# One core, two encoder layers: the order of a layer's steps written out anew, with weight steps of two units instead of four

## The chip, the cores and the metric

One core of a Trainium2 chip runs the whole program. The metric is the device time of one execution in microseconds (us), lower is better. The time before is 1046.75 us, the median of three runs (1046.62, 1046.75 and 1047.17).

The engines are named as in the profile: PE (TensorE, matrix products, with PEld for its weight loads), DVE (VectorE), ACT (ScalarE), POOL (GpSimd) and SP (SyncE, which here issues the DMAs of the weights). Each engine works through its own list of instructions in order. They meet at semaphores.

## The reference

The input x is 256 tokens by 1024 channels, float32. Two layers run one after the other, each of them:

```python
for l in range(DEPTH):                      # DEPTH = 2
    h = _rms(x, norm_g[l])
    p = einsum('bsd,de->bse', h, w_in[l])   # 1024 -> 11808 columns
    (a_qkv, a_a, a_b, a_z, b_qkv, b_z, c_q, c_k, c_v, c_z,
     d_q, d_k, d_v, d_i, d_f, d_o, d_z, gate_logits) = _split(p, PROJ_SIZES)
    y_a = gated DeltaNet, both directions, after a convolution over 5 tokens and SiLU
    y_b = attention in a neighbourhood of 16 columns, 8 heads of 64
    y_c = grouped-query attention with axial rotary, 4 heads of 128
    y_d = mLSTM, both directions
    proj = einsum('bsnw,nwd->bsnd', ys, w_branch[l])     # 4 branches, 512 -> 1024
    merged = sum over branches of sigmoid(gate_logits) * proj
    x = x + einsum('bsd,de->bse', merged, w_out[l])
```

Each mixer's output is multiplied by a SiLU gate of its own (za, zb, zc, zd). DeltaNet and mLSTM work in four chunks of 64 tokens. In DeltaNet every chunk needs the inverse of a 64x64 lower triangular matrix for each head.

## The kernel before

**Weights in units.** All weights of a layer, 232 blocks of 256 KB, are cut into "units" (`weight_plan`, line 213). SP loads a unit into one of six places of `ring` (line 1084). Since the products are made at a higher precision than one pass gives, every unit is split in two: ACT rounds it (`w_high`, line 1149) and DVE takes what is left (`w_low`, line 1475). PE then makes three products for each unit and each of two token tiles: lines 654, 655 and 656, six matmuls of 128x512 for most units. PARTS = 6 pairs of `w_high`/`w_low` exist, and LEAD = 4: a step that multiplies units k to k+n-1 on PE has ACT and DVE split units k+4 to k+n+3. Unit u can be split once unit u-6 has been used.

**Steps.** `order()` (line 127) makes one list of steps, and every engine goes through that same list (`run`, line 608), taking from each step its own part. A step ("proj", kind, arg, u, n) multiplies n units from unit u of a block on. Everything else is a small step. In the kernel before a block of eight units is made in two steps of four (SIZES = (4, 4), line 56), a branch block of four in one, and small steps lie between. The list depends on the position in `streamed`, on the integers in `add(...)` (so many weight steps here) and on `weave`, which mixes lists by fractions of a stretch. Because the list is common, the place of a small step in it sets where it stands on PE, ACT, DVE and POOL at once, and an engine that waits in one step holds up all of its later ones.

**At the end of a block** ACT and DVE have more to do (line 1212 and line 1701). After all but two of its splits ACT waits until the product of the first token tile is complete, takes it from PSUM, makes a split, waits for the second tile's product, takes it, and makes the last split. So the last split of a block's last step comes after PE has ended the whole block, and a small step that follows stands behind it on ACT and DVE. In the middle of a block nothing of this kind waits.

**The units in their order**: conv 0 to 3 are units 0 to 15, za 16 to 19 and 28 to 31, conv 4 and 5 units 20 to 27, c 32 to 47, zc 48 to 55, b 56 to 79, zb 80 to 87, d 88 to 103, o 104 to 111, zd 112 to 119, then for branches 0, 2, 1 and 3 and for two halves of the columns each a gate block of eight and a branch block of four (120 to 215), and out 216 to 231.

**Small steps that are spoken of below.**
- `conv.i`, `silu.i`: the convolution (DVE lines 1548 to 1552, ACT line 1271 and POOL lines 1951 to 1954 halve the work) and its SiLU (ACT 1277, DVE 1562). `a_turn.i` transposes the result on PE (line 648) and ACT takes it (1154).
- `gatecols`, `gatecols_turn`, `cols`: the gate columns of DeltaNet and mLSTM. gatecols_turn is a dialogue of DVE (1520 to 1540) and ACT (1253 to 1259, with a load of the table for Ln). cols: POOL makes eight copies into `sel` (line 1962), PE sums them (lines 780 to 783) once `selected` is 8, ACT takes exp, DVE makes terms (1567).
- `rope`: POOL only. Four copies (line 2043) and four products (2047) that make the rotary tables. The user is c_rotate.
- `a_norm`, `a_scale`, `a_qkt`, `a_kkqk`, `rows.s`: DeltaNet's norms and its decay matrices. rows.s is a chain PE (793), DVE (1593, 1595), ACT, POOL (1991), DVE (1597, 1599), and for s = 0 and 1 the first inverse (1612 to 1618).
- `solve0.s`, `t1.s.n`, `update.s.n`: the solve by levels n = 1 to 5, for chunks 0 and 1 together, then 2 and 3. POOL masks (2003), PE (831), ACT takes (1154), PE (842, 847), DVE subtracts (1630, at the last level 1633).
- `uw.s`, `qd.s`, `scan_v.s`, `scan_o.s`: the scan over chunks. scan_o ends with two products for the state (912) which wait until ACT has emptied the bank of the output (1154).
- `c_prep` to `c_out`: grouped attention; `c_rotate.t` is DVE work (1754 to 1767). `b_square`, `b_prep`, `b_turn_in`, `b_score`, `b_turn`, `b_mix`, `b_sum`, `b_out`: neighbourhood attention.
- `d_rows`, `d_prep`, `d_m`, `d_step.s`, `d_turn.s`, `d_scan.s`, `d_den`, `d_sum`, `d_gate`, `d_out`: mLSTM. d_step.s is DVE (1867), ACT (1415), DVE (1870). d_turn.s transposes what it makes.
- `x_out.t` puts the finished branch of x = a, b, c, d on PE for transposing; `y_parts.n` splits it as a weight is split; `merge_turn`, `merged` prepare the last product.

## Time and profile before

| | |
|---|---|
| median of three runs | 1046.75 us |
| the profiled execution, its own time | 1044.77 us |
| its span, first to last instruction | 1042.9 us |
| PE busy | 916.5 us, 88% of the span |
| DVE busy | 676.0 us, 65% |
| ACT busy | 520.7 us, 50% |
| POOL busy | 248.6 us, 24% |
| mean granted TensorE clock | 0.963 of full speed |
| weights and the rest over DMA | 140.15 MB, mean 134 GB/s |

The two layers take the same course, some 516 us apart: a row at 657 us of the second layer has its twin at about 141 us of the first. All rows below are of the second layer, whose own work begins at about 528 us. In a timeline row the first number is the start in us, the second the duration of the group, then engine, line, operation and tiles, and in brackets the idle time before it and what ended that. Half speed of TensorE's clock is 1.2 GHz, full speed 2.4 GHz.

### The profile page before, as it was taken

Reading aid. Unit: us, or ns where it says so; the run is one execution under the profiler, and the core shown is the slowest. Engines: PE = TensorE matmul, PEld = TensorE weight load, DVE = VectorE, ACT = ScalarE, POOL = GpSimd, SP = SyncE. Lnnn points to the kernel's source line nnn. Section 1 sums busy time; section 2 is a strip of 40 time slices with the busy share of each in tenths; the row PEclk is TensorE's granted clock in tenths of the full one; section 3 lists DMA queues with packets and bytes.
Section 4 is the critical chain, followed back from the end, with each engine's and each line's share of the span. In section 5 each row is a group of like instructions: output and inputs, shape, how many; then the busy total and the mean of one; then the engine's idle time right before and its main releaser. Section 6 shows DMA issues by size and latency. Waiting matters only on the chain. (4 is left out here: it accounts for less than half of the span.)

```text
span 1042.9 us, 19727 instructions
## 1 busy us (share of the span) xinstructions
PE 916.5 (88%) x7206; PEld 759.3 (73%) x7206; DVE 676.0 (65%) x1149; ACT 520.7 (50%) x1050; POOL 248.6 (24%) x264
## 2 busy tenths in 40 slices
PE   3888989989899899999858889898898989989996
PEld 3876768767777687778657877686777767877785
DVE  3877784646377576686459768654653776755773
ACT  3676544444344554545257745444443545554652
POOL 1643210413510003321024512122423100221210
PEclk9988999989999999999978999999899999999999
DMA  7634534315265244447256435434243742434662
GB/s 208 181 122 131 179 118 124 105 53 156 72 162 166 67 148 132 136 151 225 81 137 183 134 120 171 128 103 122 80 126 82 193 130 82 150 112 143 185 210 71
DMA packets 101405, 140.15 MB, mean 134 GB/s; under 512 B 31022, under 2 KB 45494, under 8 KB 101174
## 3 DMA queue, kind: packets, MB, share of 16 engines
q1 hardware_dynamic: 94118, 137.80, 44.3%
q10 hardware_dynamic: 7184, 1.02, 0.6%
q8 instruction: 60, 0.98, 0.4%
q14 instruction: 43, 0.35, 0.1%
HBM read 135.63 MB, written 7.27 MB: 137 GB/s over the span
## 5 line engine op out<-in xcount | busy, mean ns | idle before, releaser
L1475 DVE TENSOR_TENSOR w_low<-ring,w_high 128x512 fp32r<-128x512 f32 x464 | 329.7, 752 | 148.2 <-ACT w_high L1149 147.9
L1149 ACT ACTIVATE w_high<-ring 128x512 fp32r<-128x512 f32 x464 | 274.3, 627 | 98.2 <-PE pj L656 61.3
L654 PE MATMUL pj<-w_high,h_high 128*128 128x512 f32 x592 | 244.0, 412 | 24.1 <-DVE w_low L1475 16.5
L655 PE MATMUL pj<-w_low,h_high 128*128 128x512 f32 x592 | 235.9, 398 | 0.0
L656 PE MATMUL pj<-w_high,h_low 128*128 128x512 f32 x592 | 235.6, 398 | 0.0
L654 PEld LDWEIGHTS pj<-w_high,h_high 128*128 128x128 f32 x592 | 114.6, 194 | 52.4 <-issue 11.0
L656 PEld LDWEIGHTS pj<-w_high,h_low 128*128 128x128 f32 x592 | 114.2, 193 | 25.2
L655 PEld LDWEIGHTS pj<-w_low,h_high 128*128 128x128 f32 x592 | 114.7, 194 | 23.1 <-issue 0.5
L1154 ACT ACTIVATE big<-pair 128x512 f32<-128x512 f32 (+2 forms) x136 | 60.2, 481 | 56.9 <-PE pair L831 22.9
L2101 POOL TENSOR_TENSOR zbuf<-zbuf,mid 128x512 f32<-128x512 f32 x20 | 29.1, 1469 | 111.8 <-DVE mid L1908 111.7
L2003 POOL TENSOR_TENSOR big<-big,tab 128x256 f32<-128x256 f32 x40 | 31.5, 805 | 82.0 <-PE pair L831 56.8
L654 PE MATMUL mb<-w_high,h_high 128*128 128x512 f32 x112 | 44.6, 398 | 3.1 <-DVE h_low L1921 3.1
L654 PE MATMUL pj<-h_high,w_high 128*128 128x256 f32 x128 | 38.0, 297 | 6.9 <-DVE h_low L1489 6.2
L656 PE MATMUL mb<-w_high,h_low 128*128 128x512 f32 x112 | 43.7, 390 | 0.0
L655 PE MATMUL mb<-w_low,h_high 128*128 128x512 f32 x112 | 43.6, 390 | 0.0
L654 PE MATMUL pj<-w_high,y_high 128*128 128x512 f32 x88 | 35.3, 401 | 3.3 <-DVE w_low L1475 3.3
L655 PE MATMUL pj<-h_low,w_high 128*128 128x256 f32 x128 | 37.6, 293 | 0.0
L656 PE MATMUL pj<-h_high,w_low 128*128 128x256 f32 x128 | 37.4, 292 | 0.0
L648 PE MATMUL pair<-tab,big 128*128 128x128 f32 x208 | 29.5, 281 | 6.2 <-DVE big L1870 3.4
L656 PE MATMUL pj<-w_high,y_low 128*128 128x512 f32 x88 | 34.4, 390 | 0.0
L655 PE MATMUL pj<-w_low,y_high 128*128 128x512 f32 x88 | 34.3, 390 | 0.0
L1940 POOL TENSOR_SCALAR small<-small 128x8 f32<-128x8 f32 (+3 forms) x10 | 4.2, 418 | 125.1 <-ACT mid L1179 59.0
(287 smaller groups left out, 1653.8 us busy)
## 6 DMA issues: line engine op xcount, KB each, us to landing
ring<-in_w_in SPq DMA_DIRECT2D x368, 256.0 KB, 3.0
ring<-in_w_branch SPq DMA_DIRECT2D x64, 256.0 KB, 3.7
ring<-in_w_out SPq DMA_DIRECT2D x32, 256.0 KB, 3.2
big<-skew SPq DMA_DIRECT2D x32, 128.0 KB, 3.8
skew<-lines SPq DMA_DIRECT2D x16, 224.0 KB
out_x<-btm SPq DMA_DIRECT2D x12, 256.0 KB, 3.8
btm<-out_x SPq DMA_DIRECT2D x8, 256.0 KB, 4.7
tab<-in_table SPq DMA_DIRECT2D x1, 1408.0 KB, 8.1
```

Source lines behind the costliest of these rows:

```text
L648: last = tr(bank.t[0:width, k * P:(k + 1) * P], v, ident)
L654: mm(o, r32(a), r32(b), start=start, stop=False, skip_group_check=True)
L655: mm(o, r32(a), r32(b_low), start=False, stop=False, skip_group_check=True)
L656: return mm(o, r32(a_low), r32(b), start=False, stop=stop, skip_group_check=True)
L1149: f(r32(w_high[:, u % PARTS]), ring[:, u % RAW], ACT.Copy).then_inc(w_rounded, 1)
L1154: f(dst, view(bank_of(key).t), ACT.Copy, scale=scale).then_inc(bank_of(key).free, 1)
L1475: tt(r32(w_low[:, u % PARTS]), ring[:, u % RAW], w_high[:, u % PARTS], ALU.subtract).then_inc(w_split, 1)
L1940: link(pool.tensor_scalar(dst, src, scale, EPS, ALU.mult, ALU.add))
L2003: pool.tensor_tensor(sLm[:, j].rearrange("p (k h) n -> p k h n", k=2), sLT[:, j].rearrange("p (k h) n -> p k h n", k=2), both, ALU.mult)\
L2101: pool.tensor_tensor(m, m, gact[i % 2][:, t], ALU.add).then_inc(merge_done, 1)
```

## The change

The function that computed the list is gone. In its place stands the list itself, as a text, and `order()` only reads it. Three things differ in what the engines do.

1. Every block but conv is made in steps of two units. The units and their order are the same, and the order of the matmuls within a block is the same too.
2. Many small steps have another place. One place is given below as the number of units that PE has before it in the layer.
3. POOL has one more wait in `cols`: for `rope_ready` to be 4, in other words for its own step `rope`, which now comes shortly before.

| step | before | after |
|---|---|---|
| rope | 0 | 16 |
| gatecols_turn | after conv.2 and silu.1 | ahead of both |
| a_turn.0 | 20 | 16 |
| silu.4 | 28 | 24 |
| a_scale, conv.5 | 28 | 30 |
| a_kkqk, a_turn.2 | 36 | 34 |
| rows.0 | 40 | 36 |
| c_prep, solve0.0, solve0.1 | 48 | 50 |
| update.0.1, update.1.1, c_qkt | 56 | 54 |
| c_score.0.0 | 60 | 56 |
| c_mix.0.0, t1.0.3, c_score.1.0 | 64 | 62 |
| c_mix.0.1, update.0.3, c_turn.1.0 | 68 | 66 |
| c_mix.1.0, rows.3 | 72 | 70 |
| update.0.5, update.1.5 | 80 | 76, 78 |
| uw.0, uw.1 | 80, 84 | 78, 84 |
| scan_o.0 | 84, ahead of solve0.2 | 88, behind t1.2.1 |
| solve0.2, solve0.3 | 84 | 86 |
| b_prep | 96, behind t1.3.3 | 94, ahead of t1.2.3 |
| scan_o.1 | 104 | 98 |
| update.2.5, update.3.5 | right behind t1 | two units behind t1 |
| scan_v.3, scan_o.3 | 112, 112 | 110, 112 |
| b_turn_in | 128 | 116 |
| b_out.0, b_out.1 | 160, 160 | 158, 172 |
| d_step.0, d_step.1, d_turn.0 | 160, 160, 160 | 146, 160, 160 |
| d_turn.1, d_turn.3, d_scan.0 | 164, 172, 172 | 168, 170, 172 |
| d_scan.3, d_den | 184, 184 | 180, 184 |

```diff
--- before.py
+++ after.py
@@ -53,7 +53,6 @@
 CW, CK = 256, 2
 WB, CUN = 512, 4
 RAW, PARTS, LEAD = 6, 6, 4
-SIZES = (4, 4)
 
 TILE_OF = (0, 1, 1, 0)
 KIND_OF = (0, 0, 1, 1)
@@ -124,90 +123,42 @@
     return where, at
 
 
+SCHEDULE = """
+    norm conv:0:0+4 conv.0 conv:1:0+4 conv.1 silu.0 gatecols conv:2:0+4 gatecols_turn conv.2 silu.1 conv:3:0+4 conv.3 silu.2 a_turn.0 rope za:0:0+2
+    za:0:2+2 silu.3 conv:4:0+4 cols conv.4 a_turn.1 a_norm silu.4 conv:5:0+4 za:0:4+2 a_scale conv.5 za:0:6+2 silu.5 a_qkt c:0:0+2 a_kkqk a_turn.2
+    c:0:2+2 rows.0 c:0:4+2 c:0:6+2 c:1:0+2 c:1:2+2 rows.1 c:1:4+2 c:1:6+2 zc:0:0+2 c_prep solve0.0 solve0.1 zc:0:2+2 c_rotate.0 c_rotate.1 t1.0.1
+    zc:0:4+2 update.0.1 t1.1.1 update.1.1 c_qkt zc:0:6+2 c_score.0.0 rows.2 b:0:0+2 b:0:2+2 t1.0.2 t1.1.2 c_turn.0.0 c_score.0.1 update.0.2 update.1.2
+    b:0:4+2 c_mix.0.0 t1.0.3 t1.1.3 c_turn.0.1 c_score.1.0 b:0:6+2 b:1:0+2 c_mix.0.1 c_turn.1.0 update.0.3 update.1.3 c_score.1.1 t1.0.4 t1.1.4
+    b:1:2+2 b:1:4+2 c_mix.1.0 c_turn.1.1 rows.3 update.0.4 update.1.4 b:1:6+2 c_mix.1.1 b:2:0+2 t1.0.5 t1.1.5 b:2:2+2 c_sum.0 c_sum.1 update.0.5
+    b:2:4+2 update.1.5 c_out.0 uw.0 b:2:6+2 zb:0:0+2 zb:0:2+2 scan_v.0 uw.1 zb:0:4+2 qd.0 c_out.1 qd.1 solve0.2 solve0.3 zb:0:6+2 t1.2.1 scan_o.0
+    t1.3.1 update.2.1 update.3.1 b_square scan_v.1 t1.2.2 t1.3.2 d:0:0+2 update.2.2 update.3.2 d:0:2+2 d:0:4+2 b_prep t1.2.3 t1.3.3 d:0:6+2 update.2.3
+    update.3.3 d:1:0+2 t1.2.4 t1.3.4 scan_o.1 d:1:2+2 d:1:4+2 update.2.4 update.3.4 d:1:6+2 o:0:0+2 t1.2.5 t1.3.5 o:0:2+2 update.2.5 update.3.5 uw.2
+    scan_v.2 uw.3 qd.2 qd.3 scan_o.2 o:0:4+2 scan_v.3 o:0:6+2 scan_o.3 zd:0:0+2 a_sum zd:0:2+2 a_gate.0 a_gate.1 b_turn_in zd:0:4+2 zd:0:6+2 a_out.0
+    a_out.1 gate:0,0:0+2 gate:0,0:2+2 y_parts.0 gate:0,0:4+2 d_rows.0 d_rows.1 gate:0,0:6+2 branch:0,0:0+2 branch:0,0:2+2 d_rows.2 d_rows.3
+    gate:0,1:0+2 gate:0,1:2+2 d_prep b_score.0.0 b_score.0.1 b_turn.0.0 gate:0,1:4+2 gate:0,1:6+2 b_mix.0.0 b_score.1.0 b_turn.0.1 branch:0,1:0+2
+    branch:0,1:2+2 b_mix.0.1 b_score.1.1 b_turn.1.0 d_m gate:2,0:0+2 d_step.0 gate:2,0:2+2 b_mix.1.0 b_turn.1.1 y_parts.2 gate:2,0:4+2 gate:2,0:6+2
+    b_mix.1.1 b_sum.0 b_sum.1 branch:2,0:0+2 branch:2,0:2+2 gate:2,1:0+2 b_out.0 gate:2,1:2+2 d_step.1 d_turn.0 d_step.2 gate:2,1:4+2 gate:2,1:6+2
+    branch:2,1:0+2 branch:2,1:2+2 d_turn.1 d_step.3 d_turn.2 gate:1,0:0+2 d_turn.3 gate:1,0:2+2 d_scan.0 b_out.1 y_parts.1 gate:1,0:4+2 d_scan.1
+    gate:1,0:6+2 branch:1,0:0+2 d_scan.2 branch:1,0:2+2 d_scan.3 gate:1,1:0+2 gate:1,1:2+2 d_den d_sum gate:1,1:4+2 gate:1,1:6+2 branch:1,1:0+2
+    d_gate.0 d_gate.1 branch:1,1:2+2 d_out.0 d_out.1 gate:3,0:0+2 gate:3,0:2+2 y_parts.3 gate:3,0:4+2 gate:3,0:6+2 branch:3,0:0+2 branch:3,0:2+2
+    gate:3,1:0+2 gate:3,1:2+2 gate:3,1:4+2 gate:3,1:6+2 merge_turn.0 merged.0 branch:3,1:0+2 branch:3,1:2+2 out:0:0+2 out:0:2+2 merge_turn.1 merged.1
+    out:0:4+2 out:0:6+2 out:1:0+2 out:1:2+2 out:1:4+2 out:1:6+2
+"""
+
+
 def order():
 
-
-
-    def block(kind, arg, sizes):
-        at = [sum(sizes[:i]) for i in range(len(sizes))]
-        return [("proj", kind, arg, u, n) for u, n in zip(at, sizes)]
-
-    def proj(kind, n):
-        return [step for i in range(n) for step in block(kind, i, SIZES)]
-
-    def gates(n):
-        return [g for c in range(2) for g in block("gate", (n, c), SIZES) + block("branch", (n, c), (BK,))]
-
-    streamed = iter(proj("za", 1) + proj("c", 2) + proj("zc", 1) + proj("b", 3) + proj("zb", 1) + proj("d", 2)
-                    + proj("o", 1) + proj("zd", 1) + [g for n in BRANCHES for g in gates(n)])
-    o = []
-
-    def stream():
-        step = next(streamed, None)
-        if step and step[:2] == ("proj", "gate") and step[2][1] == 0 and step[3] == KT // 2:
-            o.append(("y_parts", step[2][0]))
-        if step:
-            o.append(step)
-        return step
-
...
-    add(("norm",), ("rope",), *block("conv", 0, (CUN,)), ("conv", 0), *block("conv", 1, (CUN,)), ("conv", 1), ("silu", 0), ("gatecols",),
-        *block("conv", 2, (CUN,)), ("conv", 2), ("silu", 1), ("gatecols_turn",), *block("conv", 3, (CUN,)), ("conv", 3), ("silu", 2), 1, ("a_turn", 0),
-        ("silu", 3), *block("conv", 4, (CUN,)), ("cols",), ("conv", 4), ("a_turn", 1), ("a_norm",), *block("conv", 5, (CUN,)), ("silu", 4), ("a_scale",), ("conv", 5),
-        1, ("silu", 5), ("a_qkt",), 1, ("a_kkqk",), ("a_turn", 2), 1)
-
-
...
-    groups = [(t, q) for t in range(NT) for q in range(2)]
-    attention = [("c_qkt",)]
-    for n, g in enumerate(groups):
-        attention += [("c_score", *g)] + ([("c_mix", *groups[n - 1])] if n else []) + [("c_turn", *g)]
-    attention += [("c_mix", *groups[-1]), ("c_sum", 0), ("c_sum", 1), ("c_out", 0), ("c_out", 1)]
-
...
-    add(("rows", 0), 1, ("rows", 1), 1, *weave((solve(0), 0, 1), ([("c_prep",), ("c_rotate", 0), ("c_rotate", 1)], 0, 0.15), (attention, 0.25, 1), ([("rows", 2), ("rows", 3)], 0.1, 0.95), ([1] * 8, 0, 1)),
-        ("uw", 0), 1, ("uw", 1), ("qd", 0), ("scan_v", 0), ("qd", 1), ("scan_o", 0))
-    add(*weave((solve(2), 0, 1), ([("scan_v", 1), ("scan_o", 1)], 0, 1), ([("b_square",), ("b_prep",)], 0.05, 0.75), ([1] * 6, 0.2, 0.9)))
-    add(("uw", 2), ("scan_v", 2), ("uw", 3), ("qd", 2), ("qd", 3), ("scan_o", 2), 1, ("scan_v", 3),
-        ("scan_o", 3), ("a_sum",), 1, ("a_gate", 0), ("a_gate", 1), 1, ("a_out", 0), ("a_out", 1), 2)
-
-    add(("b_turn_in",), ("d_rows", 0), ("d_rows", 1), 1, ("d_rows", 2), ("d_rows", 3), 1, ("d_prep",), ("b_score", *groups[0]), ("b_score", *groups[1]))
-    for n, g in enumerate(groups):
-        add(("b_turn", *g), 1, ("b_mix", *g))
-        if n + 2 < len(groups):
-            add(("b_score", *groups[n + 2]))
-        if n == 1:
-            add(("d_m",))
-    add(("b_sum", 0), ("b_sum", 1), 2, ("b_out", 0), ("b_out", 1))
-
-    add(("d_step", 0), ("d_step", 1), ("d_turn", 0), 1, ("d_step", 2), ("d_turn", 1), 1, ("d_step", 3), ("d_turn", 2), 1, ("d_turn", 3))
-    add(("d_scan", 0), 1, ("d_scan", 1), 1, ("d_scan", 2), 1, ("d_scan", 3), ("d_den",), ("d_sum",), 1, ("d_gate", 0), ("d_gate", 1), 1, ("d_out", 0), ("d_out", 1))
-    while stream():
-        pass
-
-    last = proj("out", 2)
-    half = len(SIZES) // 2
-    return o[:-1] + [("merge_turn", 0), ("merged", 0), o[-1]] + last[:half] + [("merge_turn", 1), ("merged", 1)] + last[half:]
+    steps = []
+    for word in SCHEDULE.split():
+        if ":" in word:
+            kind, arg, span = word.split(":")
+            arg = tuple(map(int, arg.split(",")))
+            u, n = map(int, span.split("+"))
+            steps.append(("proj", kind, arg if len(arg) > 1 else arg[0], u, n))
+        else:
+            name, *args = word.split(".")
+            steps.append((name, *map(int, args)))
+    return steps
 
 
 def weight_plan(stages):
@@ -1956,6 +1907,7 @@
 
                     def cols():
                         pool.wait_ge(gates_ready, 2)
+                        pool.wait_ge(rope_ready, 4)
                         for s in range(STEPS):
                             for half in range(2):
                                 d = half ^ KIND_OF[s]
```

## Rows read from the trace of the kernel before

**Rows 1.** The page, busy time of each engine over the span.
```profile
PE 916.5 (88%) x7206; PEld 759.3 (73%) x7206; DVE 676.0 (65%) x1149; ACT 520.7 (50%) x1050; POOL 248.6 (24%) x264
```

**Rows 2.** The stages of the second layer: start:end, length, then busy us by engine.
```profile
core 0: us, PE busy (x) PEld busy (x) DVE busy (x) ACT busy (x) POOL busy (x), PEclk, DMA share, GB/s
528.00:607.00 79.00, 63.11 (x423) 58.84 (x423) 64.93 (x118) 51.89 (x111) 36.99 (x47) 0.88 0.51 147
607.00:657.00 50.00, 45.41 (x424) 36.64 (x424) 38.18 (x78) 26.11 (x52) 7.39 (x8) 0.97 0.53 162
657.00:731.00 74.00, 67.19 (x718) 55.44 (x720) 40.09 (x66) 33.14 (x73) 17.49 (x18) 1.00 0.39 116
731.00:742.00 11.00, 7.88 (x203) 6.94 (x194) 6.00 (x13) 5.56 (x12) 2.86 (x4) 0.69 0.01 3
742.00:813.00 71.00, 64.39 (x753) 52.30 (x754) 36.53 (x53) 26.20 (x51) 24.24 (x20) 1.00 0.43 120
813.00:905.00 92.00, 87.55 (x452) 69.92 (x452) 67.49 (x124) 51.10 (x111) 7.46 (x9) 0.98 0.46 128
905.00:976.00 71.00, 65.23 (x385) 52.23 (x384) 46.98 (x72) 35.70 (x68) 20.71 (x20) 0.98 0.43 132
...
```

**Rows 3.** Timeline of PE in the front: two long waits, cols, two matmuls in a row.
```profile
569.53 0.76 PE L654 MATMUL pj<-w_high,h_high 128*128 128x512 f32 x1 [4.20 <-DVE w_low L1475]
...
583.82 0.29 PE L780 MATMUL mb<-small,tab 128*128 128x16 f32 x2
...
599.63 0.39 PE L656 MATMUL pj<-w_high,h_low 128*128 128x512 f32 x1
599.86 0.39 PE L654 MATMUL pj<-w_high,h_high 128*128 128x512 f32 x1
...
607.45 0.50 PE L654 MATMUL pj<-w_high,h_high 128*128 128x512 f32 x1 [3.64 <-DVE zbuf L1694]
```

**Rows 4.** Timeline of POOL in the front: rope, and the copies of cols (right behind conv.3).
```profile
537.32 1.95 POOL L2043 COPY mid<-mid 128x64 f32<-128x64 f32 x4 [8.12 <-DMA small<-in_ml_i_bias]
539.35 4.06 POOL L2047 TENSOR_TENSOR mid<-tab,mid 128x256 f32<-128x256 f32 x4
...
576.40 3.82 POOL L1962 COPY small<-small 64x16 f32<-64x16 f32 x8
```

**Rows 5.** Timeline of DVE: the split of a weight, POOL idle, and POOL busy.
```profile
558.86 1.28 DVE L1475 TENSOR_TENSOR w_low<-ring,w_high 128x512 fp32r<-128x512 f32 x2
...
910.11 1.10 DVE L1475 TENSOR_TENSOR w_low<-ring,w_high 128x512 fp32r<-128x512 f32 x1
```

**Rows 6.** Timeline of PE, attention, solve and scan: waits of PE.
```profile
666.57 0.66 PE L648 MATMUL mb<-tab,mid 128*128 128x128 f32 x4 [1.73 <-ACT mid L1367]
...
677.87 1.10 PE L934 MATMUL mb<-mid 128*128 128x256 f32 x4 [0.60 <-DVE mid L1780]
...
707.49 0.66 PE L648 MATMUL mb<-tab,mid 128*128 128x128 f32 x4 [1.41 <-DVE mid L1681]
...
733.37 0.46 PE L817 MATMUL pair<-tab,big 64*64 64x64 f32 x16 [1.78 <-DVE big L1618]
...
810.68 1.09 PE L898 MATMUL mb<-big 128*64 128x128 f32 x16 [1.70 <-DVE big L1641]
```

**Rows 7.** Timeline of DVE: first and last instruction of c_rotate, and scan_o.0.
```profile
643.19 1.22 DVE L1754 TENSOR_TENSOR mid<-mid 128x512 f32<-128x512 f32 x1
...
651.92 0.96 DVE L1767 TENSOR_TENSOR mid<-mid,small 128x768 f32<-128x768 f32 x1
...
730.74 1.29 DVE L1650 COPY big<-mb 128x512 f32<-128x512 f32 x2 [6.07 <-PE mb L912]
```

**Rows 8.** Timeline of PE among the gates: two waits.
```profile
915.33 1.09 PE L648 MATMUL pair<-tab,big 128*128 128x128 f32 x4 [1.71 <-DVE big L1870]
...
969.20 0.47 PE L654 MATMUL pj<-w_high,y_high 128*128 128x512 f32 x1 [1.67 <-DVE w_low L1475]
```

**Rows 9.** Two stretches with TensorE's clock down, columns as in rows 2.
```profile
734.00:742.00 8.00, 6.66 (x151) 5.85 (x144) 3.15 (x5) 5.53 (x12) 2.86 (x4) 0.57 0.02 4
...
915.00:923.00 8.00, 7.67 (x29) 6.29 (x30) 2.94 (x6) 3.54 (x7) 0.00 (x0) 0.79 0.21 66
```

16 lines of the change are left out of this document (removed).

## The prediction

> **What bounds the kernel now.** I read the page's busy times first. PE is busy for 916.5 of 1042.9 us, and the next engine, DVE, for 676.0 [rows 1]. The change adds and removes no arithmetic, so PE's work stays, and what an order can give back is PE's idle time, 126 us for two layers, and the time in which PE works at half clock. Second, I read the table of stages of layer two, where length less PE busy is PE's idle time [rows 2]: 15.9 us in the front (528 to 607), 4.6 us from 607 to 657, 6.8 us in attention and first solve (657 to 731), 3.1 us in the eleven us at the start of the second solve, 6.6 us to the end of the scan (813), 4.5 us from 813 to 905, 5.8 us from 905 to 976. The tail behind 976 is not touched but for steps of two, and I count nothing there. Third, the timeline of PE tells who ended each wait: hardly ever a DMA, mostly DVE or ACT work of a small step whose input was made just before [rows 3, 6, 8]. DVE is at 54 to 76% behind 607 [rows 2]. So the waits are latencies and not a second full engine: the answer of ACT or DVE is short, and PE has nothing to do in between since the next step in the list is the one that needs the answer. They go if one pair of units stands between question and answer. Matmuls of a block start 0.23 us apart [rows 3], so a unit with its six is 1.4 us of PE, a pair 2.8 us, and four units 5.6 us. Waits under 1 us have no row of their own here; they are what a stage's idle time holds besides the longer ones.
>
> **The change part by part.** I followed the new list through each engine from the same moment on.
>
> *The front (units 0 to 33).* Taking rope out of the start frees POOL there, while DVE makes the first splits, a gain of at most some 0.5 us a layer. It is put behind conv.3 on POOL, and all of its instructions count: 1.95 + 4.06 = 6.0 us [rows 4]. POOL ends conv.3 at 576.3 and then makes the eight copies of cols in 3.8 us, done at 580.2, while PE asks for them only at 583.8 [rows 3, 4]. With rope between, the copies end at 576.3 + 6.0 + 3.8 = 586.2, so PE stands before cols for up to 2.4 us. Behind cols on PE are a_turn.1 and conv 5, on DVE conv.4, a_norm, and all splits from unit 28 on. The added wait for rope_ready comes after POOL's own rope and costs only the 0.1 us of one completion. gatecols_turn before conv.2 moves the same DVE and ACT work ahead, and the splits of units 16 to 19 behind it end when they did: the 4.20 us wait stays but for a_turn.0, 1 us of PE work that is now done inside it: 0.5 us gained. silu.4 ahead of the splits of units 28 to 31 makes za's second half start some 2 us later. What then sets the start of c is DVE's chain a_norm, a_scale, conv.5, the splits and za's gate, which ended the 3.64 us wait at 607.45 [rows 3]. It starts 1.2 us later, because of cols, but two splits (2 x 0.64 us, [rows 5]) are now made inside its wait for POOL's root and not between conv.5 and the gate: 1.3 us less. The sum is that c starts when it did. Two of the idle times become one shorter and one longer. I take 0 for the front, between +3 (PE's wait for cols comes on top) and -2 (less time at half clock).
>
> *A rule against this move.* The splits of DVE take 0.64 us with POOL idle and 1.10 us with POOL at work [rows 5], and rope's four products now run while DVE splits units 20 to 27. The Trainium skill says the same as a rule (GPSIMD Engine Reference, its table of the engine's properties): POOL's way to SBUF is shared with VectorE, with contention for DVE instructions that have two SBUF inputs, and a split has two. By it the four products (4.06 us, [rows 4]) slow four to six splits, some 2 us of DVE a layer, 4 us in all. I count none of it, since DVE waits for cols in any case at that place; if it were on the path the sum would be 4 us worse.
>
> *607 to 657.* rows.0 four units earlier lets its chain over DVE, ACT and POOL run beside c's second half. The two c_rotate, 9.7 us of DVE from 643.19 to 652.88 [rows 7], still end after PE asks for c_qkt, though two units and update are moved ahead: so what PE waited in front of c_qkt and rows.2 turns into some 1.6 us in front of c_qkt, and t1.0.1 waits some 1 us longer for c_prep's root on POOL. The wait of under 1 us for a split behind rows.0 goes. Of 4.6 us idle I take 1 us as gained.
>
> *657 to 731, 6.8 us idle.* The exp of c_score.0.0 had only t1 to hide in, and PE waited 1.73 us; now four units stand between. c_mix.0.0 stood at the end of a block: its DVE part was queued behind the last split, which waits for the block's last product, so that PE waited 0.60 us; now it stands in mid-block. c_out.0 waited 1.41 us for c_sum, which now is four units ahead [rows 6]. Of the same kind are smaller ones (rows.3 and c_mix.1.1, uw.0 behind update, qd.1 behind uw.1). What stays is the wait of scan_o.0's second half for ACT to empty its bank, 0.8 us, wherever scan_o stands. Some 0.2 us are the sum of what the timeline doesn't name. Gain 6.8 - 1.0 = 5.8 us.
>
> *731 to 742, 3.1 us idle.* DVE was stopped in scan_o.0 until 730.74, 6 us of it idle, and only then made the inverse on which solve0.2 waited 1.78 us [rows 6, 7]. With scan_o.0 behind solve0, DVE makes it while PE is in zb. The masks of t1.2.1 get two units as well. One new wait of 0.2 us or so is left in update.3.1. Gain 2.9 us. Besides, 734 to 742 ran at a mean clock of 0.57 of full speed, behind this group of waits: 6.66 us busy, of which 6.66 x 0.43 = 2.9 us would not be there at 2.4 GHz [rows 9]. I take it as gained, with 0 as the other end, since the waits that put the clock down may come together elsewhere.
>
> *742 to 813, 6.6 us idle.* Moved apart are t1.x.3 and update, t1.x.5 and update.2.5 (each under 1 us, 1.3 together), and scan_v.3 from scan_o.2 (1.70 us, [rows 6]), 3.0 us; uw.2 to scan_o.2 are as before, with the other 3.6 us. b_prep on POOL, with the long root in it, is now ahead of the masks of t1.2.3, which by my reckoning are ready 1 to 2 us before PE asks. Gain 2.8 us.
>
> *813 to 905, 4.5 us idle.* d_prep and b_score keep theirs. b_turn_in moves with its own wait. ACT's takes of b_turn.1.0 are no longer behind d_m. Gain 0.5 us.
>
> *905 to 976, 5.8 us idle.* b_out.0 and b_out.1 no longer share a bank back to back (0.8 us). d_turn.0 finds d_step.0 made fourteen units earlier (1.71, [rows 8]), and the low clock behind this wait, 7.67 x 0.21 = 1.6 us [rows 9], should go with it. d_scan.0 is two units behind d_turn.3 (1 us). d_den comes four units after d_scan.3 and not right behind it, so that DVE's chain starts before PE gets there, and the split it held up, 1.67 us [rows 8], is in time. Gain 0.8 + 1.7 + 1.0 + 1.7 = 5.2 us, less 0.1 us, and 1.5 us of clock, 6.6 us.
>
> **The sum.** Per layer 0 + 1 + 5.8 + 5.8 + 2.8 + 0.5 + 6.6 = 22.5 us. An order with eighty changed neighbourhoods makes small waits I have not seen; I take one seventh off, to 19.3 us, and for two layers 38 us (the first layer's stages follow the same course). The profiled execution took 1044.8 us, of which the span is 1042.9 us, so it would become some 1006.5 us. It lies 2.0 us under the median of the runs, 1046.75, which gives 1008.5 us as the time to expect.
>
> **The rivals.**
> 1. *Half of the stalls come back.* What is idle on PE is also what ACT and DVE use to catch up. In attention DVE is at 54% and ACT at 45%, which speaks against it, while in the front DVE is at 82% and from 813 to 905 at 73% [rows 2], which speaks for it. If half of the 19.3 us returns as new waits for DVE, the time is 1046.75 - 19 = 1028 us.
> 2. *Slower: the lead of four units runs out.* Splits are queued in the list between small steps, and PE has four units, 5.6 us, when a small step starts. Wherever DVE's or POOL's chain in small steps exceeds this, PE waits for a split. Such chains are c_rotate (9.7 us, [rows 7]), b_prep with the root before it, d_den with d_sum, rows.0 and rope (6.0 us, [rows 4]). It decides from 22 us of new waits a layer on. With some eight such places at 3.5 us, 28 us, less the 22.5 us won, two layers become 11 us slower: 1058 us. Against it: the lead is four units in both kernels, the chains are the same ones, and before only the 1.67 us [rows 8] and one of 0.6 us were of this kind behind the front.
> 3. *The change does not do what it says.* If PE's order were tied down by something else than the list, for instance by the arrival of weights, nothing would change, 1046 us. Of the waits read, none behind the front was ended by a DMA.
> 4. *Everything comes true and the front gains too*: 22.5 x 2 and 2 x 2 for clock, 998 us.
>
> **How the numbers follow.** The forecast (1000 to 1018 us) has 0.52, rival 1 (1018 to 1040) 0.26, rival 4 0.10, rival 3 0.04, rival 2 0.08. The predicted time is 1008.5 us. The range for 8 in 10 reaches from 1000 into rival 1, to 1034 us. 0.2% is 2 us, about what a measurement of this kernel can tell from no change. Faster by more has 0.89, the same 0.04, slower 0.07.
>
> **What would show it.** In the trace of the changed kernel: PE's idle time in the second solve under 1.5 us and no wait at L817; no wait in front of d_turn.0 and d_scan.0; a new wait of 1 to 2.5 us at L780, ended by POOL; the 0.79 us at L912 still there; c starting within 2 us of where it did, counted from the layer's start. The prediction is wrong if waits of L654 for w_low, now 1.67 and 0.6 us behind the front, grow past 10 us a layer, or if the granted clock is lower than 0.963 in the mean.

## The result, and the profile after

The median of four runs is 988.68 us (986.53 to 989.64), against 1046.96 us for the kernel before in the same session: a ratio of 0.944 [0.941, 0.947], 58 us less. The forecast was 1008.5 us and a gain of 38 us, and the measured time lies under the low end of the range. The profiled execution took 988.89 us, its span is 987.1 us, and its mean granted clock 0.978 of full speed (before 0.963). Busy times after, to be held against [rows 1]:

```profile
PE 902.7 (91%) x7206; PEld 750.6 (76%) x7206; DVE 675.9 (68%) x1149; ACT 520.2 (53%) x1050; POOL 246.8 (25%) x264
```

PE does the same 7206 matmuls in 13.8 us less. The busy times of DVE, ACT and POOL stay within 2 us, so this part is the clock. The rest of the gain is idle time of PE, 84.4 us where it was 126.4.

To see where, the second layer is cut at the same units in both kernels: units 0, 32 (start of c), 60, 76, 88 (start of d), 112 (start of zd), 132, 144 (start of the gates of branch 2), 192 (gates of branch 3) and 212. First before, then after; columns as in [rows 2].

```profile
537.40:608.00 70.60, 59.34 (x407) 55.39 (x407) 60.76 (x112) 50.23 (x106) 36.02 (x45) 0.91 0.46 138
608.00:670.10 62.10, 56.00 (x559) 45.31 (x558) 46.13 (x91) 30.82 (x67) 11.22 (x13) 0.97 0.52 161
670.10:708.40 38.30, 35.62 (x379) 29.80 (x378) 22.64 (x39) 17.02 (x39) 8.72 (x9) 1.00 0.37 109
708.40:748.80 40.40, 35.12 (x454) 28.83 (x454) 19.04 (x31) 18.23 (x36) 8.46 (x9) 0.92 0.25 74
748.80:813.30 64.50, 57.88 (x698) 47.11 (x697) 31.98 (x46) 24.25 (x47) 23.57 (x20) 1.00 0.45 124
813.30:848.30 35.00, 33.83 (x154) 26.57 (x153) 27.54 (x41) 20.20 (x36) 7.07 (x7) 1.00 0.67 173
848.30:884.80 36.50, 33.79 (x193) 26.43 (x192) 24.53 (x41) 17.40 (x46) 0.00 (x0) 0.95 0.30 93
884.80:977.10 92.30, 85.83 (x498) 69.84 (x497) 63.51 (x117) 49.20 (x98) 21.10 (x22) 0.98 0.43 130
977.10:1005.20 28.10, 28.10 (x130) 23.34 (x129) 18.58 (x25) 15.55 (x27) 6.01 (x4) 1.00 0.77 233
```

```profile
510.90:580.40 69.50, 61.20 (x407) 56.89 (x407) 60.99 (x112) 49.10 (x104) 35.32 (x45) 0.88 0.49 146
580.40:637.80 57.40, 54.04 (x559) 44.18 (x558) 46.12 (x91) 31.21 (x64) 11.55 (x13) 1.00 0.51 155
637.80:673.70 35.90, 35.90 (x392) 29.68 (x391) 23.56 (x42) 18.87 (x44) 9.20 (x9) 1.00 0.45 136
673.70:706.30 32.60, 31.81 (x441) 26.45 (x440) 16.53 (x30) 17.61 (x36) 7.71 (x9) 1.00 0.35 106
706.30:768.30 62.00, 58.38 (x697) 46.84 (x697) 33.59 (x46) 23.60 (x46) 24.42 (x19) 1.00 0.40 110
768.30:802.30 34.00, 33.66 (x154) 26.57 (x154) 27.79 (x41) 19.97 (x36) 7.08 (x7) 1.00 0.72 200
802.30:837.20 34.90, 32.19 (x193) 25.51 (x192) 24.27 (x41) 17.29 (x46) 0.00 (x0) 1.00 0.30 92
837.20:921.20 84.00, 83.22 (x498) 68.61 (x497) 62.98 (x116) 49.30 (x98) 21.17 (x22) 1.00 0.48 146
921.20:949.30 28.10, 28.10 (x129) 23.35 (x128) 18.58 (x24) 15.55 (x27) 5.99 (x4) 1.00 0.74 225
```

Length less PE busy is PE's idle time. Read in pairs, the second layer became 29.4 us shorter (467.8 to 438.4), the first, cut alike, 28.1 us (468.8 to 440.7). Between unit 212 of the first layer and unit 0 of the second the changed kernel takes 1.4 us more (47.8 to 49.2), and the two profiled executions are 55.9 us apart. The table is for the second layer:

| units | length | idle | PE busy (clock) |
|---|---|---|---|
| 0 to 32, front | -1.1 | 11.3 to 8.3 | +1.9 |
| 32 to 60, c and zc | -4.7 | 6.1 to 3.4 | -2.0 |
| 60 to 76, attention | -2.4 | 2.7 to 0 | +0.3 |
| 76 to 88, second solve starts | -7.8 | 5.3 to 0.8 | -3.3 |
| 88 to 112, scan | -2.5 | 6.6 to 3.6 | +0.5 |
| 112 to 132 | -1.0 | 1.2 to 0.3 | -0.2 |
| 132 to 144, b_score | -1.6 | 2.7 to 2.7 | -1.6 |
| 144 to 192, gates, d | -8.3 | 6.5 to 0.8 | -2.6 |

Of the 3.3 us of the second solve some 0.5 are 13 matmuls that now stand before unit 76; the clock itself gave 2.8.

PE's timeline after names what is left. A row per kind, the idle time and who ended it in the brackets (a_turn.0, cols, the splits of za's second half, c_qkt, a bank in scan_o, the scan of chunk 2, b_score, d_out.1; L599 transposes, L605 is the first of the three products):

```profile
541.82 1.97 PE L599 MATMUL pair<-tab,big 128*128 128x128 f32 x8 [3.52 <-DVE big L1513]
...
557.77 0.40 PE L731 MATMUL mb<-small,tab 128*128 128x16 f32 x2 [0.83 <-POOL small L1914]
...
569.81 0.79 PE L605 MATMUL pj<-w_high,h_high 128*128 128x512 f32 x1 [3.86 <-DVE w_low L1426]
...
623.29 0.88 PE L599 MATMUL mb<-tab,mid 128*128 128x128 f32 x6 [1.60 <-DVE mid L1718]
...
727.56 1.16 PE L863 MATMUL mb<-big 64*128 64x128 f32 x16 [0.79 <-ACT big L1105]
...
749.75 1.09 PE L836 MATMUL mb<-big 128*64 128x128 f32 x16 [1.19 <-ACT big L1280]
...
813.44 0.47 PE L916 MATMUL pair<-window_r,eye_r 128*128 128x512 f32 x1 [0.87 <-DVE mid L1767]
...
920.26 0.63 PE L599 MATMUL mb<-tab,big 128*128 128x128 f32 x4 [0.78 <-ACT big L1105]
```

The wait of 1.78 us for the inverse, the 1.73 us for the exp, both of c_mix and c_out [rows 6] and the two among the gates [rows 8] have no successor. No new wait of a split stands anywhere behind the front.

### The profile page after: what moved, and what is told of

It reads as the page before. It is cut to its first block and busy times, and to the rows that moved or that the text cites. A ratio compares the mean times of both kernels' runs of the same rounds, so it can differ in the third digit from the quotient of the medians.

```text
span 987.1 us, 19727 instructions
## 1 busy us (share of the span) xinstructions
PE 902.7 (91%) x7206; PEld 750.6 (76%) x7206; DVE 675.9 (68%) x1149; ACT 520.2 (53%) x1050; POOL 246.8 (25%) x264
## 5 line engine op out<-in xcount | busy, mean ns | idle before, releaser
L605 PE MATMUL pj<-w_high,h_high 128*128 128x512 f32 x592 | 244.8, 414 | 8.8 <-DVE w_low L1426 6.2
L605 PEld LDWEIGHTS pj<-w_high,h_high 128*128 128x128 f32 x592 | 113.1, 191 | 36.6 <-DVE w_low L1426 6.9
L1105 ACT ACTIVATE big<-pair 128x512 f32<-128x512 f32 (+2 forms) x136 | 60.7, 481 | 76.3 <-PE pair L782 37.1
L605 PE MATMUL mb<-w_high,h_high 128*128 128x512 f32 x112 | 44.4, 397 | 3.1 <-DVE h_low L1872 3.1
L1955 POOL TENSOR_TENSOR big<-big,tab 128x256 f32<-128x256 f32 x40 | 34.6, 882 | 48.6 <-ACT big L1270 25.0
L605 PE MATMUL pj<-h_high,w_high 128*128 128x256 f32 x128 | 38.4, 300 | 6.8 <-DVE h_low L1440 6.8
L599 PE MATMUL pair<-tab,big 128*128 128x128 f32 x208 | 30.4, 292 | 8.4 <-DVE big L1513 7.0
L605 PE MATMUL pj<-w_high,y_high 128*128 128x512 f32 x88 | 35.2, 400 | 0.0
L599 PEld LDWEIGHTS pair<-tab,big 128*128 128x128 f32 x208 | 25.7, 151 | 11.7 <-DVE big L1513 7.4
```

What stands on the lines that cost most here:

```text
L599: last = tr(bank.t[0:width, k * P:(k + 1) * P], v, ident)
L605: mm(o, r32(a), r32(b), start=start, stop=False, skip_group_check=True)
L1105: f(dst, view(bank_of(key).t), ACT.Copy, scale=scale).then_inc(bank_of(key).free, 1)
L1955: pool.tensor_tensor(sLm[:, j].rearrange("p (k h) n -> p k h n", k=2), sLT[:, j].rearrange("p (k h) n -> p k h n", k=2), both, ALU.mult)\
```

## The experiments

Each kernel was traced in one execution, so a statement on a stage is one on that execution; the medians are of all.

Two theories stood against each other. The first: every wait is a latency with its own place, worth its own length, and the places add. The second: what is taken out of one place comes back at another, or only the clock's state matters. Stage lengths below are cut at the same units as above.

### Grain or order

`old_in_pairs` keeps the old order and only cuts the fours:

```diff
-        stages = order()
+        stages = halves(order())    # each weight step of four as two of two, nothing between
```

> The old order with every step of four units cut into two steps of two that stand next to each other; no small step moves. If the gain comes from where the small steps stand, as the prediction says, this is the old kernel: 1047 us, within 3. If the size of the steps is what helps (ACT and DVE less tied to the progress of PE), it takes at least half of the 58 us: 1018 us or less.

1048.55 us, ratio 1.000 [0.998, 1.002]. The cut does nothing by itself.

`new_in_fours` does the opposite in the new list: two steps of two with nothing between them become one of four.

> The changed kernel with every pair of weight steps of two, between which no small step stands, made as one step of four again; all places stay. If the steps of two are only a means to stand between small steps: 988.7 us, within 2 us. If shorter steps help by themselves (splits asked for earlier, an end of a block that comes sooner): 3 us or more slower.

987.84 us, 0.944 [0.942, 0.946], the same as the changed kernel within the noise. `new_rounded` goes one step on. Of the 274 steps of a layer 61 stand in the middle of a four, and each is moved to the four's end:

```diff
-        stages = order()
+        stages = rounded(order())   # "c:0:0+2 a_kkqk a_turn.2 c:0:2+2" becomes "c:0:0+4 a_kkqk a_turn.2"
```

> The changed kernel's list with the weight steps in fours: 61 of its 274 steps stand behind the first two units of a four, and each of these is moved two units back, to the four's end. The places in the middle of a four are what the steps of two are for. If they matter, questions and answers of the solve and the attention meet in one gap again and the waits under 1 us come back: about 12 such meetings a layer at 0.7 to 1 us, some 10 us per layer, 1009 us (1000 to 1018). The rival, that the order alone carries the gain and the grain doesn't: under 993.

1044.22 us, 0.998 [0.997, 0.999]: all but 2 us of the gain is gone, 35 us more than expected. Busy times, the front of layer two, and three of PE's waits:

```profile
PE 919.2 (88%) x7206; PEld 764.9 (73%) x7206; DVE 678.0 (65%) x1149; ACT 522.8 (50%) x1050; POOL 246.3 (24%) x264
```

```profile
537.60:612.00 74.40, 62.91 (x409) 59.11 (x408) 62.76 (x114) 47.78 (x101) 35.74 (x45) 0.87 0.49 144
```

```profile
607.66 3.67 PE L614 MATMUL pair<-tab,big 128*128 128x128 f32 x16 [4.35 <-DVE big L1547]
...
649.72 0.48 PE L797 MATMUL pair<-big 64*64 64x64 f32 x16 [3.30 <-POOL big L1970]
...
971.53 1.12 PE L614 MATMUL mb<-tab,big 128*128 128x128 f32 x4 [4.74 <-DVE big L1647]
```

The expectation reckoned with waits under 1 us. But where two units between a question and its answer vanish, PE waits for a whole chain: a_scale, now right ahead of a_qkt (4.35), solve0 with c_prep's root before t1 (3.30), d_gate right ahead of d_out (4.74). PE busy is up by 16.5 us against the changed kernel, so all of the clock's gain (13.8) is gone too. The move is a crude one: it also makes waits that the kernel before did not have. The front takes 74.4 us (before 70.6, changed 69.5) and units 144 to 212 take 122.1 (before 120.4, changed 112.1), some 10 us of new loss in two layers. The second solve keeps more than half of its gain (34.9 us) and attention half (37.1), while scan and b_score are back where they were (64.6, 36.5). So this list needs its places in the middle of a four. What the best order in fours could give isn't shown; by these stages, an estimate, the old front and the old end alone would make it some 12 us.

### One place at a time

`old_scan_o_late` is the old order with scan_o.0 behind t1.2.1 and nothing else; `new_scan_o_early` the new order with scan_o.0 back ahead of solve0.2.

```diff
-    ... qd.1 solve0.2 solve0.3 zb:0:6+2 t1.2.1 scan_o.0
+    ... qd.1 scan_o.0 solve0.2 solve0.3 zb:0:6+2 t1.2.1
```

> The old order with one step moved: scan_o.0 behind t1.2.1. In the new order the same move the other way round cost 10 us. If what a step is worth does not hang on its surroundings, this gives 4.5 to 5 us a layer: 1038 us. If the other waits close by (uw.0, qd.1 and the masks of t1, under 1 us each) keep the clock down by themselves, only the wait of 1.8 us goes: 1043 to 1044 us.

> The new order with scan_o.0 alone put back ahead of solve0.2. The prediction's mechanism (DVE is stopped in scan_o.0 and makes the inverse late) gives back the wait of 1.8 us in front of the last part of solve0.2 and the low clock behind it, 2.9 us a layer: 988.7 + 2 x 4.7 = 998 us. If the clock stays up, because the other waits around it are gone, only the wait comes back: 992 us. If the order around it has made it harmless: 989 us.

Old with it late: 1034.36 us, 0.988 [0.984, 0.993], 11 us faster. New with it early: 998.55 us, 0.953 [0.951, 0.955], 10 us slower than the change. One place moves the time by about a sixth of the whole. Units 76 to 88, first `old_scan_o_late` in layer two, then `new_scan_o_early` in layers one and two, and its wait:

```profile
707.50:742.90 35.40, 32.28 (x453) 26.62 (x453) 19.05 (x31) 18.16 (x36) 8.41 (x9) 1.00 0.29 85
```

```profile
184.80:222.90 38.10, 34.08 (x441) 27.84 (x440) 17.21 (x31) 17.63 (x36) 8.09 (x9) 0.96 0.31 92
679.10:715.60 36.50, 32.47 (x441) 26.66 (x440) 17.18 (x30) 17.67 (x36) 8.10 (x9) 1.00 0.33 99
```

```profile
705.55 0.46 PE L768 MATMUL pair<-tab,big 64*64 64x64 f32 x16 [1.78 <-DVE big L1569]
```

The 1.78 us are those of [rows 6] to the last digit. In the old order the stage goes from 40.4 to 35.4 us, 2.2 of them idle time and 2.8 clock (35.12 to 32.28 us busy); units 32 to 60 gave 2.8 us of it back by their clock, at the same idle time (62.1 to 65.0), and b_score had its full clock in both layers (35.0 us), though nothing near it moved. The traced execution was the slowest of the four (1037.26 us), so its stages show some 7 of the 11 us. In the new order the same waits, 4.0 us in both layers, cost half clock in the first layer and none in the second: 34.08 against 32.47 us of PE for the same work. The expected 998 us was met, but by another sum: 1.8 us of waiting and 2.9 of clock a layer were expected, and the stage shows 3.2 us more idle time, 2.3 and 0.7 of clock, and 1.6 more in b_score, which fell back to half clock in both layers. That part was luck.

`new_b_turn_in_late` and `new_d_step_late` put one step back to the moved place of before (b_turn_in from unit 116 to 128, d_step.0 from 146 to 160):

> The new order with b_turn_in alone put back behind gate 0,0, ahead of d_prep and b_score. From 813 to 905 us the old trace had a stretch at half clock behind the waits of d_prep and b_score, the new one has the same waits and no such stretch. If b_turn_in's place is the reason (its own wait stood close before), this gives it back: 0.6 us of wait and 1.5 to 2 us of clock a layer, 993 us. If the clock is up for another reason, 989 to 990 us.

> The new order with d_step.0 alone put back beside d_step.1, right ahead of d_turn.0. By the prediction this gives back the wait of 1.7 us in front of d_turn.0, and with it the low clock behind, 1.5 us: 988.7 + 2 x 3.2 = 995 us. If the clock stays up, because the wait stands alone now (b_out.1 is elsewhere), 992 us.

b_turn_in: 995.22 us, 0.951 [0.949, 0.953], 6.5 us slower than the change. d_step: 994.09 us, 0.951 [0.947, 0.955], about 5 us slower. The first kernel's stage 112 to 132 (34.0 us in the changed kernel) and waits, and the second's stage 144 to 192 and wait:

```profile
770.20:806.90 36.70, 34.03 (x153) 26.51 (x152) 28.22 (x41) 20.16 (x36) 7.07 (x7) 1.00 0.70 189
```

```profile
781.83 0.65 PE L599 MATMUL pair<-tab,big 128*128 128x128 f32 x4 [0.61 <-DVE big L1632]
...
783.63 0.50 PE L605 MATMUL pj<-w_high,h_high 128*128 128x512 f32 x1 [1.15 <-DVE zbuf L1645]
...
798.35 1.06 PE L599 MATMUL pair<-tab,btm 128*128 128x128 f32 x8 [0.91 <-ACT big L1105]
```

```profile
839.20:926.00 86.80, 83.44 (x497) 68.59 (x496) 62.42 (x116) 49.60 (x98) 21.09 (x22) 1.00 0.46 140
```

```profile
868.49 0.66 PE L599 MATMUL pair<-tab,big 128*128 128x128 f32 x4 [2.58 <-DVE big L1821]
```

Without b_turn_in between a_gate and a_out, PE comes to a_out 0.61 us before DVE has ended a_gate, and to the next product 1.15 us before its bank is empty, and b_turn_in itself waits 0.91 us where it waited 0.34. The stage has 2.7 us of idle time where it had 0.3, and b_score is at half clock again in both layers (36.5 us). With d_step.0 late the wait in front of d_turn.0 is back, 2.58 us long where it was 1.71 [rows 8]. PE may get there sooner; that isn't shown. The clock did not come down with it: PE is busy 83.44 us in the stage, against 83.22 in the changed kernel, where the expectation had 1.5 us of clock.

`new_rope_first` puts rope back at the layer's start and takes the added wait out:

```diff
-    norm conv:0:0+4 ...  a_turn.0 rope za:0:0+2
+    norm rope conv:0:0+4 ...  a_turn.0 za:0:0+2
-                        pool.wait_ge(rope_ready, 4)
```

> The new order with rope back at the start and without the added wait. In the trace of the changed kernel PE waits 0.83 us in front of cols in the second layer, ended by POOL. If that is all that rope costs, this is 1 to 3 us faster, 986 to 988 us. If the late cols also hold the whole chain of DVE up to the start of c, as the prediction had it (1.2 to 2.4 us a layer), 984 to 986 us. If rope at the start costs more there, by sharing POOL's and DVE's way to SBUF with the first splits, it is slower: 990 us or more.

987.20 us, 0.943 [0.941, 0.944], 1 to 2 us less than the change, which the intervals don't tell apart from it. The front is 68.6 and 68.2 us long against 70.9 and 69.5, so rope's move costs 1.3 to 2.3 us a layer. The other traces bear this out: with rope behind a_turn.0 and the front otherwise as in the changed kernel the 18 fronts of nine kernels take 69.4 to 70.9 us, and with rope elsewhere the six of three kernels 67.5 to 68.6. But b_score's half clock comes back in both layers (36.5 us) and takes 3 us of it.

### Part by part

`new_to_c` is the new order to a_qkt and the old one behind; `new_to_scan_end` the new order to scan_o.3, the old one from a_sum on.

> The new order up to a_qkt (32 units), the old one behind it, in steps of four. The prediction gave the front nothing, between +3 and -2 us a layer: 1041 to 1053 us, with 1047 as its value. The two traces show c start 0.7 and 1.1 us earlier, and 1 us more won by the fortieth unit, where the new one is at full clock: 1043 to 1045 us by them.

> The new order from the layer's start through scan_o.3, the old order from a_sum on. By the stages of the two profiles the part through scan_o.3 gives 0.7 to 1.0 (rope, start) + 3.9 to 4.7 (projections) + 2.4 (rows, columns) + 7.7 (solve, split) + 2.5 (scan) = 17.5 to 18.3 us per layer, so about 1010.5 us (1008 to 1014). The theory that waits are worth their own time wherever they stand: this number. The rival, that the later part's gain depends on the earlier one (its waits shrink when the engines come to them earlier): under 1005. The earlier run with the new order only up to a_qkt (1039) against this one gives the share of the solve and scan: about 18 x 2 - 8 = 28 us.

To c: 1039.23 us, 0.994 [0.991, 0.996], 4 to 9 us of gain. The stages give the front 1.8 us in two layers (2.3 in this kernel's own trace), and its profiled execution (1045.55 us) was its slowest, so no trace shows where the rest was; this stays open. To the scan's end: 1006.20 us, 0.961 [0.957, 0.965]. That is 40 us of the 58, and the sum of the two layers' stages gives the same (21.4 and 18.9 us), 37 us of it in units 0 to 112 and 3 in b_score, which had its full clock in this kernel already, in the old order. The last part, 17.5 us, answers to the last stages of the table (2 x 8.3 and 2 x 1.0).

Idle time bears out the first theory: in every kernel traced, a stage behind the front in which no step has moved has the idle time of the list that it comes from, within some 0.1 us, whatever was moved elsewhere (3.6 us in the scan in the new order, 6.6 in the old one). The clock does not add in this way. It came back elsewhere in `old_scan_o_late` and `new_scan_o_early`, so that part of the second theory stands.

### What puts the clock down

In b_score the waits are the same four before and after (0.25, 0.83, 0.87 and 0.76 us), 2.7 us in all, yet before PE needs 33.79 us and after 32.19 us. `new_shift_8` and `new_shift_16` repeat a_out's transposes, 8 or 16 a layer, twelve units ahead of this stage:

```diff
+                        for _ in range(1 if name == "a" else 0):      # 2 in new_shift_16
+                            for k in range(BK):
+                                tr(bank.t[:, k * P:(k + 1) * P], y_tile[name][t][:, k * P:(k + 1) * P], ident)
```

> The changed kernel with 8 of a_out's transposes repeated in each layer, on TensorE alone: about 0.9 us of work per layer and nothing else. Work alone: 988.7 + 1.8 = 990.5 us. If the half clock at b_score depends on the moment at which its waits come, it may return here though the waits are the same (2.7 us): stage 132 to 144 then 36.5 instead of 34.9 us, and 993.7 us in all. If it hangs on the waits' length alone, the stage stays at 34.9.

> As the kernel before it with 16 repeated transposes, 1.8 us of work per layer: 992.3 us by work alone, 995.5 with the half clock in b_score in both layers. The theory of the moment: at least one of the two kernels shows 36.5 us in stage 132 to 144 in at least one layer, at 2.7 us of waits. The rival (length alone): neither does.

991.53 us, 0.947 [0.943, 0.950], and 993.14 us, 0.949 [0.945, 0.952]. Units 132 to 144 in layers one and two, first with 8, then with 16 more; and the last wait of the stage with 8 more, in the layer with half clock (328) and in the one without (818):

```profile
315.70:352.20 36.50, 33.79 (x193) 26.84 (x192) 24.26 (x41) 17.51 (x46) 0.00 (x0) 0.95 0.29 88
805.90:840.90 35.00, 32.29 (x194) 25.53 (x193) 24.36 (x41) 17.29 (x46) 0.00 (x0) 1.00 0.30 93
```

```profile
315.40:350.30 34.90, 32.19 (x193) 25.53 (x192) 24.27 (x41) 17.30 (x46) 0.00 (x0) 1.00 0.29 91
804.90:841.50 36.60, 33.89 (x194) 26.79 (x193) 24.40 (x42) 17.52 (x46) 0.00 (x0) 0.95 0.30 90
```

```profile
328.06 0.51 PE L919 MATMUL pair<-window_r,eye_r 128*128 128x512 f32 x1 [0.76 <-DVE mid L1770]
...
818.33 0.51 PE L919 MATMUL pair<-window_r,eye_r 128*128 128x512 f32 x1 [0.76 <-DVE mid L1770]
```

Same kernel, same waits to the hundredth, and half clock in one layer only. The length of the waits doesn't decide it alone. That their moment does is argued, not shown: no run holds all else fixed, and with one traced execution each it isn't shown either that the repeated transposes brought the half clock back. The Trainium skill has a rule that fits (TensorE: Matmul & The Clock Gate, What's actually happening): the window in which TensorE's activity is judged is free-running and does not start anew with the kernel, so that the point of the clock's change varies. These traces agree with it as far as they go: 1.6 us a layer, there or not.

### Two kernels beyond the change

`better_a` puts rope behind silu.5, moves the last level of the solve ahead of o's first units, parts d_out.0 from d_out.1, puts merge_turn.1 ahead of out's second step, and brings t1.0.1 behind two more units:

```diff
-    c_rotate.1 t1.0.1 zc:0:4+2 update.0.1 t1.1.1 update.1.1 c_qkt zc:0:6+2 c_score.0.0 rows.2
+    c_rotate.1 zc:0:4+2 t1.0.1 t1.1.1 zc:0:6+2 update.0.1 update.1.1 c_qkt rows.2 b:0:0+2 c_score.0.0
-    d:1:6+2 o:0:0+2 t1.2.5 t1.3.5 o:0:2+2 update.2.5 update.3.5 uw.2 scan_v.2
+    d:1:6+2 t1.2.5 t1.3.5 o:0:0+2 update.2.5 update.3.5 uw.2 o:0:2+2 scan_v.2
```

`better_b` is the same without the first pair of lines.

> The new order with the same rule used on waits that are left: rope behind silu.5; t1.1.1 and both updates and c_qkt a pair of units further from what they wait for; a pair of units between uw.2 and scan_v.2 and between d_out.0 and d_out.1; merge_turn.1 ahead of a pair of units of out. The waits in question are 0.8, 3.4, 1.3, 0.8 and 1.6 us a layer, 7.9 us. If they go and nothing new comes, 988.7 - 15.8 = 973 us. If DVE is by now too full to answer in time, half or less: 981 us or more.

> The changed kernel with the rope's steps first, o's waits in the scan moved away and d's last steps one place on; without the edit of the projections that cost a wait of 3.42 us. By the stages of the run that had all of them: 2.0 us at the front, 1.1 in 88 to 112, 1.5 in 144 to 192, 4.5 us per layer, less what the clock takes back at b_score (1.6 per layer, in three of the runs): 980 us without it, 983 with it. The rival, that only the clock's state matters by now: 986 to 990.

988.83 us, 0.945 [0.941, 0.950], and 980.44 us, 0.937 [0.933, 0.940]. By the medians the first pair of lines cost what the others gained. Its trace has a new wait: rows.2 stands right behind c_qkt, and DVE comes to the update that it needs only at 620.99 us, behind c_rotate and the end of zc's block.

```profile
621.81 0.67 PE L744 MATMUL pair<-big,tab 128*128 128x256 f32 x2 [3.42 <-DVE big L1581]
```

This is part of the cost only. Units 32 to 60 take 61.1 and 60.5 us in `better_a` and 57.9 in both layers of `better_b`: 1.0 us a layer more idle time, since other waits fell, and 2.3 and 1.5 us of clock. Besides, the traced execution of `better_a` (982.61 us) was by far its fastest. The other four took 987.8 to 989.3 us, at a mean clock of 0.967 and 0.968 where it had 0.977, and what they lost there no trace shows.

`better_b` in layer two: the scan (88 to 112), 60.9 us where the changed kernel takes 62.0; then units 144 to 212 and what is behind 212, first in the changed kernel, then in `better_b`:

```profile
698.50:759.40 60.90, 58.48 (x697) 46.72 (x696) 34.77 (x46) 23.49 (x46) 24.86 (x19) 1.00 0.42 112
```

```profile
837.20:949.30 112.10, 111.32 (x625) 91.95 (x624) 81.56 (x139) 64.85 (x124) 27.16 (x26) 1.00 0.54 166
949.30:987.10 37.80, 28.14 (x127) 22.82 (x125) 18.21 (x29) 11.59 (x20) 0.00 (x0) 0.92 0.34 112
```

```profile
829.90:941.80 111.90, 111.41 (x626) 91.85 (x625) 81.80 (x140) 64.56 (x124) 27.14 (x26) 1.00 0.54 166
941.80:977.70 35.90, 27.81 (x127) 22.76 (x125) 18.28 (x29) 11.45 (x20) 0.00 (x0) 0.94 0.37 118
```

The scan gives 1.1 us, merge_turn.1 ahead of out's second step 1.9, since a wait of 1.57 us goes, and parting d_out.0 from d_out.1 only 0.2: units 144 to 192 are shorter (82.5 against 84.0 us), but d_out.1 with its wait now stands behind them. The front gives 3.4 and 1.0 us, and b_score lost its full clock in layer two, 1.6 us.

By the ratios better_b is 8 us faster than the changed kernel, and by the medians of its session it is 66 us faster than the kernel before.

## Why the prediction came out too small

Sign, mechanism and places were right; the size was 20 us short, 10.1 us a layer set against layer two: 4.5 by the clock, 3.2 by the seventh taken off, 1.3 by idle time and 1.1 by the front. No single term explains the miss. Without the seventh the sum gives 1002 us, with the clock as measured 999, with both 993. By the prediction's own terms:

- **One seventh off the sum, 3.2 us a layer: this step failed.** It was a sum for waits not seen, and none came: the idle time outside the front was forecast to fall by 18.1 us (22.5 less 4.4 of clock) and fell by 19.4 (31.0 to 11.6). Nothing in the rows asked for the discount.
- **The clock: this step failed too, and it is the larger one, 4.4 against 8.9 us outside the front.** I counted it only where I had drawn a window over it [rows 9]. c's start (2.0) and b_score (1.6) were also partly at half clock before, as the 0.97 and 0.98 in [rows 2] say, and I put them at nothing without a reason. The solve gave 2.8 (3.3 with the moved matmuls) where I had 2.9, the gates 2.6 where I had 1.5. The 1.6 us of b_score are not tied to anything in the change: its waits are the same, and other kernels show either clock. That part of the gain was luck. The front took 1.9 back. PE busy, 13.8 us less over the span, is the check: 4.4 a layer could never give it.
- **Idle time behind the front, right within 1.3 us.** By stages: units 32 to 88 gave 9.9 us, forecast 1 + 5.8 + 2.9 = 9.7 (c_qkt's new wait of 1.60 us and the 0.79 us in scan_o were forecast as 1.6 and 0.8); the scan 3.0, forecast 2.8; behind 112 6.5, forecast 0.5 + 5.1 = 5.6.
- **b_turn_in "moves with its own wait", counted at nothing.** Put back, it costs 2.3 us of idle time a layer, with b_score's clock down as well, and 6.5 us in all by the medians: its work on PE is what covers a_gate's answer.
- **The front, 0 forecast, between +3 and -2.** It gave 0.7 and 1.1 us. PE waits 0.83 us for cols, forecast 1 to 2.5 us and so somewhat less, and c starts within 2 us of where it did. What it hides is shown by `new_rope_first`: rope's new place costs 1.3 to 2.3 us a layer, which the rest of the front makes good.
- **The rule on POOL and DVE.** The prediction had rope's four products beside four to six splits, at 2 us of DVE a layer. Four splits ran beside rope, in 3.15 us, but three of them beside its copies, 0.64 us from start to start. Only the fourth met the products and took 1.23 us, where one with POOL idle takes 0.64 [rows 5]. The Trainium skill's rule (GPSIMD Engine Reference, its table of the engine's properties) has contention for DVE instructions with two SBUF inputs, and on this one split the trace agrees, at some 0.6 us. DVE then sits 3.15 us idle until ACT answers, so it costs nothing here, as I took it. POOL's rope, then DVE, after, with the fourth split by itself between:

```profile
548.25 2.11 POOL L1995 COPY mid<-mid 128x64 f32<-128x64 f32 x4
550.44 3.71 POOL L1999 TENSOR_TENSOR mid<-tab,mid 128x256 f32<-128x256 f32 x4
```

```profile
548.90 3.15 DVE L1426 TENSOR_TENSOR w_low<-ring,w_high 128x512 fp32r<-128x512 f32 x4
...
550.83 1.23 DVE L1426 TENSOR_TENSOR w_low<-ring,w_high 128x512 fp32r<-128x512 f32 x1
...
560.06 0.17 DVE L1518 TENSOR_SCALAR small<-small 128x16 f32<-128x16 f32 x1 [3.15 <-ACT small L1235]
```

- **Rivals.** Half of the stalls coming back (1028) is refuted by PE's idle time, which fell by 19.4 us outside the front where 18.1 were forecast. That the change does nothing (1046) is refuted by the time. The lead of four units ran out nowhere behind the front: no wait of a split stands there, and the 1.67 us [rows 8] is gone. The nearest case was rival 4, all true and the front gains too, at 998 us. It was still 9 us too high, by the clock.
- **Small slips, without weight.** DVE is at 51% from 742 to 813 us [rows 2], not at 54% or more. Two layers of 19.3 us are 38.6, not 38. The chances of a faster kernel add to 0.88, not 0.89.

The terms as measured, front 1.1, idle 19.4 and clock 8.9, make 29.4 us for layer two, and with 28.1 for layer one 57.5 us. (19.4 + 8.9 = 28.3.) Less the 1.4 us between the layers and 0.2 at the two ends these are the 55.9 us between the two profiled executions; the medians are 58.3 us apart. Why the stretch between the layers grew stays open: PE waits 4.05 us for DVE there, in front of the second layer's first product, where it waited 3.32.

## What to carry to other kernels

Where one engine bounds a kernel and every engine goes through one common list, read each of its waits as the time from a question to its answer, and give each just one piece of independent work, small enough to stand between any two small steps. Here the cut alone was worth nothing and both together 58 us; the new list rounded to the old grain was worth 2 us, with some 10 us of waits that the rounding itself made. Take such waits at their full length when nothing in the rows shows an engine too busy to answer; a part taken off for the unseen had nothing under it here. Count the clock over the whole span, from stages at less than full clock wherever they are, not only at the wait one is looking at; and check the result by the busy time of the engine, whose work stayed the same. Expect idle time to add from place to place, and the clock's share not to. Before a stage is called shorter, see whether a step has left it.
